# Order of the expert passes: where the wide couples of narrow experts stand among the single experts

## The reference

```
logits = h @ router_w + router_b                 # 1024 rows x 32 experts
experts, weights = best two of the best group    # 2 per row, 2048 assignments
expert_block(xb, e): (silu(xb @ w1[e]) * (xb @ w3[e])) @ w2[e]   # w1, w3: 1024x512, w2: 512x1024
out[row] = sum over its two experts of weight * expert_block(row)
```

## Time and profile before

| | |
|---|---|
| time, median of three runs | 1092.22 us (1091.91 to 1094.1) |
| span of the profiled execution | 1092.7 us |
| TensorE busy | 987.7 us, 90% |
| VectorE busy | 545.4 us, 50% |
| ScalarE busy | 353.4 us, 32% |
| DMA, mean over the span | 271 GB/s |
| transfers of expert weights | 96 of 2048 KB |

### The profile page before, as it was taken

The page is one execution under the profiler, slowest core; times in us unless marked ns, Lnnn a source line. Parts: engine busy times, 40 slices in busy tenths (PEclk is TensorE's granted clock), DMA queues, the critical chain, the costliest instruction groups (busy, mean ns, idle before and its releaser), DMA issues.

```text
span 1092.7 us, 12936 instructions
## 1 busy us (share of the span) xinstructions
PE 987.7 (90%) x5014; PEld 676.3 (62%) x5014; DVE 545.4 (50%) x850; ACT 353.4 (32%) x525; POOL 127.2 (12%) x131
## 2 busy tenths in 40 slices
PE   3799999999999999975999999999899989988853
PEld 2477888888889688864675546454545355445521
DVE  2588643514653456555864536343634264334526
ACT  5521025322222443333652234222513233224112
POOL 2000000001210002212030221020100111010102
PEclk9899899999999999975999999999999999999977
DMA  9829511111303373358999999999999999998555
GB/s 369 297 93 340 202 40 39 39 39 40 117 1 136 116 273 97 113 194 219 335 366 369 417 426 427 427 426 425 427 428 426 427 426 411 423 423 361 227 241 230
DMA packets 52319, 295.82 MB, mean 271 GB/s; under 512 B 10889, under 2 KB 23194, under 8 KB 35874
## 3 DMA queue, kind: packets, MB, share of 16 engines
q1 hardware_dynamic: 43682, 274.00, 63.7%
q0 software_dynamic: 7424, 16.80, 4.0%
q10 hardware_dynamic: 1152, 4.19, 0.9%
HBM read 278.03 MB, written 25.33 MB: 278 GB/s over the span
## 4 chain that ended last, share of the span: by engine, by line
PE 66%; DMA 17%; DVE 8%; ACT 3%; issue 2%; DVEq 1%; POOL 1%; ACTq 0%; SPq 0%; POOLq 0%
DMA place_dt_float<-in_exp_w_dram 14%; PE bank L1144 7%; PE bank L1125 7%; PE bank L1120 4%; PE bank L823 4%; PE bank L818 4%; DVE place_dt_float32r L1975 4%; PE bank L820 4%; PE bank L819 4%; PE bank L824 3%; PE bank L825 3%; PE bank L1114 3%; PE bank L1117 3%; PE bank L992 2%; PE bank L995 2%
## 5 line engine op out<-in xcount | busy, mean ns | idle before, releaser
L1975 DVE TENSOR_TENSOR place_dt_float32r<-place_dt_float,place_dt_float32r 128x4096 fp32r<-128x4096 f32 x32 | 141.4, 4419 | 72.6 <-ACT place_dt_float32r L1421 72.6
L1421 ACT CAST place_dt_float32r<-place_dt_float 128x4096 fp32r<-128x4096 f32 x32 | 115.6, 3613 | 168.9 <-DMA place_dt_float<-in_exp_w_dram 147.2
L1144 PE MATMUL bank<-place_dt_float,arena 128*128 128x512 f32 x256 | 115.4, 604 | 1.7 <-issue 1.7
L1125 PE MATMUL bank<-place_dt_float,tail_dt_float 128*64 128x512 f32 x512 | 113.4, 595 | 2.3 <-DMA place_dt_float<-in_exp_w_dram 2.3
L719 POOL DMA_INDIRECT y_dram<-arena,slot_i x24 | 54.1, 2253 | 442.3 <-DVE arena L1986 442.3
L823 PE MATMUL bank<-low_r 128*128 128x256 f32 (+1 forms) x320 | 93.7, 293 | 0.0
L825 PE MATMUL bank<-low_r 128*128 128x256 f32 (+1 forms) x320 | 90.8, 284 | 0.0
L824 PE MATMUL bank<-low_r 128*128 128x256 f32 (+1 forms) x320 | 90.7, 284 | 0.0
L1114 PE MATMUL bank<-place_dt_float32r,tail_dt_float32r 128*128 128x512 f32 x256 | 70.3, 417 | 15.7 <-ACT place_dt_float32r L1421 12.8
L1144 PEld LDWEIGHTS bank<-place_dt_float,arena 128*128 128x128 f32 x256 | 47.9, 192 | 58.0 <-issue 56.7
L818 PE MATMUL bank<-low_r 128*128 128x512 f32 x192 | 78.5, 409 | 4.8 <-DVE arena L1582 3.6
(11 more groups left out here) (271 smaller groups left out, 1546.7 us busy)
## 6 DMA issues: line engine op xcount, KB each, us to landing
place_dt_float<-in_exp_w_dram SPq DMA_DIRECT2D x96, 2048.0 KB, 28.6
arena<-in_w_ada_dram SPq DMA_DIRECT2D x24, 1024.0 KB, 9.1
low<-in_w_in_dram SPq DMA_DIRECT2D x11, 1024.0 KB, 5.5
arena<-y_dram SPq DMA_DIRECT2D x8, 1024.0 KB, 7.4
arena<-in_x_dram SPq DMA_DIRECT2D x2, 2048.0 KB, 7.8
wout_dt_float<-in_w_out_dram SPq DMA_DIRECT2D x2, 2048.0 KB, 7.9
arena<-in_x_dram SPq DMA_DIRECT2D x8, 512.0 KB, 3.5
x_dram<-arena SPq DMA_DIRECT2D x8, 512.0 KB, 3.5
```

Source lines behind the costliest of these rows:

```text
L1125: mm = pe.matmul(out_[rows_, :], x[:, k, rows_], w[:, k, :], start=(k == 0), stop=(k == KD - 1))
L1144: mm = pe.matmul(bank[5 + j][:], hT_sb[:, k, :], ws[0][:, k, cols], start=(k == 0), stop=(k == KF - 1))
L1421: act.copy(part_hi[0 if kind == "w1" else 1], alias[F32][n % SLOTS]).then_inc(S["w_hi"], 1)
L1975: TT(alias[F32R][n], alias[F32][n], part_hi[j].bitcast(F32), ALU.subtract).then_inc(S["w_lo"], 1)
```

## The change

With S for a single and C for a couple, the 24 passes were in the order SSSSC SC SSC SC SSC SC SSC SC SS. The spaces are only for reading. They are now in the order SSSC SSC SSC SSC SSC SSC SSC SC. The 16 singles and the 8 couples keep their own order, and the last pass is now a couple. The order of loads, `stream`, follows from `passes` by itself, and so do the gathers, scatters and all counts to wait for.

```diff
-    passes = singles[:4]
+    passes, done = [], 0
     for q in range(COUPLES):
-
-        a, b = [4 + (WIDE - 4) * n // COUPLES for n in (q, q + 1)]
-        passes += [(WIDE + q, WIDE + COUPLES + q)] + singles[a:b]
+        upto = min(FIXED + 2 * q, WIDE)
+        passes += singles[done:upto] + [(WIDE + q, WIDE + COUPLES + q)]
+        done = upto
+    passes[-1:-1] = singles[done:]
```

## The result

| | before | after |
|---|---|---|
| median | 1092.56 us (1091.91 to 1094.1, 4 runs) | 1083.3 us (1081.81 to 1084.11, 4 runs) |
| span of the profiled execution | 1092.7 us | 1080.0 us |
| ratio of the times | | 0.9911, 95% interval 0.9891 to 0.9931 |

A forecast was written before the change was run, and what follows sets the result against it. Expert stage bound by TensorE first, then mostly by loads, then TensorE again. 1092.7 - 14.4 + 0.5 + 1.5 = 1080.3, less 0.5 (median below span) and 0.3 (front), gives 1079.5 us; own range 1074.5 to 1082, with the first rival to 1087.

The forecast's parts named there:

- The step that I called the weakest: Expert stage: loads stay the limit, so each unit lands when the same-numbered unit landed before, unit 95 at 1021.9 us.
- the 1.5 less 1.2 us of the prediction: Front of the stage: 1.5 us won from idle DMA time, less 1.2 us for an additional scatter before the last unit.
- the one more scatter: Output leaves earlier, so another scatter of 0.52 MB goes through before the last unit, costing 1.2 us.
- The steps from unit 90 to the last `down`: Tail: unit 90 lands 996.5, couple's `up` w1, turn, `down` of pass 22, `up` w3, last `down` from 1021.9 to 1029.0 us.
- 14.4 less 0.5: Tail: last `down` ends 14.4 us sooner, at 1029.0 instead of 1043.4, less 0.5 us for its partly half clock.
- the half clock in the last `down`: Last `down`: part of it may run at 1.2 GHz instead of 2.4, costing 0 to 1.7 us; 0.5 taken.
- a sign of being wrong: From 996 us on: a granted clock below 0.9 was listed among the signs that would show the prediction wrong.
- a rival for the whole stretch from 996 us on: Slower, by the clock: idle TensorE halves the clock, four products take 28 us more, up to 1108 us; chance 0.03.
- the last scatter's collision with the residual load: End of the stage: last scatter leaves about 1031 beside residual rows and gain, costing 0 to 3.4 us; 1.5 taken.
- the final stage, taken as unchanged: Behind the last scatter: the final stage's 44 us stay as before.
- The forecast's own range: Whole kernel: 1074.5 to 1082 us, from all to none of the front's gain and both small costs at their bounds; chance 0.82.
- the first rival: Tail's end held up by scatter collision, clock fall and unit 95 landing 2 to 3 us late: 1082 to 1088 us; chance 0.12.

The follow-up runs named there:

- the repetition: The changed kernel run once more with no edit, against the kernel before: ratio 0.989 (0.9861 to 0.992), 1082.45 us against 1094.01.
- The fillings: Changed kernel plus unread matmuls on TensorE in the gaps after the last `up`: with seven 1084.43 us (0.9938), with three 1081.26 us (0.9893).
- the kernel with the couples early: Changed kernel with two couples moved forward and groups of three singles late, order SSSC SC SC SSC SSC SSSC SSSC SC: 1082.87 us, ratio 0.9909.
- old-then-C S C kernel: Kernel before with its first 18 passes kept, then S S S C S C: 1083.51 us, ratio 0.9922 (0.99 to 0.9943).
- tail-only kernel: Kernel before with only the last couple moved to the end, so it ends S S S C: 1087.74 us, ratio 0.9945 (0.9926 to 0.9964).

## Why the prediction was right

**The limits.** The stage is bound by the loads until they end, and then by what TensorE has left. This held: DMA was full from 600 us on, and unit 95 landed 501.6 and 501.1 us after the issue of unit 8, against 501.1 before. The step that I called the weakest, unit n lands when unit n did, was right to half a microsecond. That this is so close is luck: kernels with one and the same order spread over 2 us in it.

**The front.** In unit 20's landing the new front gained 0.9 and 1.4 us (86.9 and 86.4 us after the issue of unit 8, before 87.8). All profiles with the front SSSCSS have 85.6 to 87.0 us there, and those with the old one 87.8 to 89.3. At unit 95 nothing was left of it that can be told, which agrees with the 1.5 less 1.2 us of the prediction. That the one more scatter took it back isn't shown.

**The tail.** The steps from unit 90 to the last `down` came in the forecast order. The forecast for the last `down` was a start at the landing, 1021.9. It started at 1020.32 and in the repetition at 1022.19, each time within 0.1 us of the landing. Before, the last product ended 21.1 us after unit 95 landed, and now 10.2 and 8.5 us after it. That is 10.9 and 12.6 us gained, where 13.9 were forecast (14.4 less 0.5). That the end C S C does this, and neither the front nor the last couple alone, is shown by the order that keeps the old front and middle, and by the one that ends S S S C.

**What was mis-sized.** The forecast gain of 12.7 us was 1 to 3 us too large, and these terms were off:
- the half clock in the last `down`. The prediction put it at 0 to 1.7 us and took 0.5, "as TensorE now idles little before it". It measured 3.0 us in the one profile and 1.4 in the other. TensorE idles 2.9 us there. The fillings speak for this as the cause, and the kernel with the couples early, with as much idle time and a full clock, against idle time alone. From 996 us to the end of the last product the granted clock was 0.90, just at the bound that the prediction had named as a sign of being wrong. The Trainium skill, "TensorE: Matmul & The Clock Gate", section "Why this matters for your kernels", says to keep idle gaps between matmuls short lest the clock drop. The trace agrees only in part: the clock fell after gaps of 0.8 and 2.1 us, both shorter than those that the page warns of, and in another kernel it held after such gaps. I had given this rule to a rival for the whole stretch from 996 us on, and it came true only in the last `down`.
- the last scatter's collision with the residual load. I took 1.5 us, and it took 3.20 us against 3.19, so nothing. The residual rows had landed by 1016.0 and the gain at 1031.95, 0.6 us before the scatter was issued. Where the scatter went out while the gain was still on its way, it took up to 4.8 us, 1.6 us more, about half of the bound of 3.4.
- the final stage, taken as unchanged. It was 44.2 and 45.1 us, before 43.8. Why is open; it lies within the spread of all profiles (43.8 to 45.3).
- the base. I set the forecast against 1092.2 us. Over all comparisons the medians of the kernel before are 1092.56 to 1094.01. This is chance of up to 2 us, which the range has to hold.

**The range.** The forecast's own range, 1074.5 to 1082, doesn't hold the measured 1083.3 or the 1082.45 of the repetition. They lie in the stretch that the first rival added. That range isn't what its bounds add up to, either. With none of the front's gain and both costs at their upper bounds the sum is 1079.5 + 1.5 + 1.2 + 1.9 = 1084.1, and with all 6.4 us of it, 4.9 more than taken, and no costs 1079.5 - 4.9 - 0.5 - 1.5 = 1072.6. Summed so, it would have held the result.

**The rivals.** None came true as a whole. Of the first one a part did, the clock, and the time fell into its stretch of 1082 to 1088. Unit 95 was not late and the scatter was not held up.

## What to carry to other kernels

Where loads bind a stage, look at what the last units are for. The backlog of compute that stands behind the last landing is paid in full, so put the work that asks for most bytes per microsecond of compute last, and a piece like it shortly before, so that the engine has caught up. Order costs nothing in bytes, and the gain is bounded by that backlog: read from the profile how long after its landing the last unit is used. When you split a product to start it early, check first whether its parts ran at the same time.

## What the runs showed of the hardware

- Matmuls of two 64-column halves, issued in turn, take 7.09 us for 32, and issued one half after the other 12.29 us at the same granted clock, 1.00.
- TensorE idle for 0.8 and 2.1 us within 3 us was followed by a granted clock of one half, and a `down` of 10.08 in place of 7.09 us. In the old-then-C S C kernel idle times of 0.8 and 1.4 us were not, and with the couples early 0.8 and 2.2 us were not either.
- The 16 DMA engines don't finish a unit together. In the profile after, the first reports unit 95 at 999.6 us and the last at 1020.2 us, and only the last one lets TensorE begin. For unit 8 the same profile has 530.4 and 532.5 us: the spread grew from 2 to 21 us in the stage.
- One execution differs from the next by up to 8.4 us in time (1083.49 to 1091.87 us, the tail-only kernel). In the profiles the issue of unit 8 alone, ahead of the change, lies between 518.0 and 521.5 us.
